# Expert stage: four token blocks by fetched rows and six dense, the low parts of u and v made on VectorE

## The chip, the cores and the metric

One of the eight cores of a Trainium2 chip runs the whole program, in fp32. Its engines are TensorE (PE; its weight loads are PEld), VectorE (DVE), ScalarE (ACT), GpSimd (POOL) and the queue of SyncE (SP) that issues transfers. The metric is the device time of one execution in microseconds (us), lower is better; the time before is the median of three runs.

## What is computed

An encoder block on 1280 tokens (256 of one request, 1024 of another) with 1024 features: norm, one projection, a two-way state-space branch, differential attention, a mix, and then PEER experts. The change is in the last part, whose reference is

```python
q = (xb @ w_q).reshape(tb, PEER_HEADS, 2, PEER_D_KEY // 2)          # 8 heads, 2 halves
s = jnp.einsum("thmd,mkd->thmk", q, sub_keys).astype(jnp.float32)   # 2 x 128 keys
s_top, i_top = lax.top_k(s, K)                                      # K = 16
...
best, pos = lax.top_k(cand, K)          # 16 of the 256 sums of a head
expert = jnp.take_along_axis(cand_idx, pos, axis=-1)                # one of 16384
gate = jax.nn.softmax(best, axis=-1)
ue = u[expert]
h = jax.nn.gelu(jnp.einsum("thkd,td->thk", ue, xb), approximate=False)
w = (gate * h).astype(xb.dtype)
return jnp.einsum("thk,thkd->td", w, v[expert])
```

Each token thus uses 8 x 16 = 128 of the 16384 experts; an expert is a row of u and a row of v, 1024 numbers each.

## The kernel before

The stages run one after another: `project`, `ssd`, `attention`, `mix`, `route` (finds each token's experts and gates), `spread_gates` and `experts`. The tokens are ten blocks of 128. In `experts` they are served in two ways side by side.

**Fetched rows.** The first `GB` = 3 blocks: for each of a token's 128 slots GpSimd issues an indirect DMA (`fetch`, L2363) that brings each of 128 tokens its own row, 128 x 1024 floats (512 KB), into one of `RB` = 6 buffers `row`. In the first half of the stage the rows are of u and VectorE makes a dot product of each with the token (`dot`, L2499); in the second half they are of v and VectorE adds each, weighted, to the token's result in `tok` (`blend`, L2510). 384 fetches for u and 384 for v.

**Dense.** The other `DB` = 7 blocks, `TD` = 896 tokens, go through all 16384 experts, 128 (one key k) at a time, two keys to a *period*, so 64 periods. TensorE multiplies u by x into `ph` (L2396), ScalarE takes the gelu (L2311), VectorE multiplies by the gates (`weights`, L2475), and TensorE multiplies that by v (`second_product`, L2418), into one of four banks `po`, 128 tokens x 512 features at a time (a *tile*, 14 to a period); VectorE adds the bank to `acc` (`add_output`, L2493). Two tiles of one block (`HELD`) stay in their own bank `held` over all periods. A period has four *quarters*: two keys by two spans of the tokens, of 512 and 384.

**Three products for one.** Each fp32 operand is split into a high part, which ScalarE rounds off by a copy (`split_u` L2294, `split_v` L2298, L2318 for w), and a low part, the rest, by a subtraction. Hence a first product of 8 x 3 matmuls a quarter and a tile of 2 x 3. The low parts of u and v are made by GpSimd (`rest_u` L2349, `rest_v` L2354: 128x1024 each, two of each per period), those of w by VectorE (`rest`, L2482). Each of u and v has one raw buffer (`u_raw`, `v_raw`): SP issues the next load (L2231, L2234) only when the low part is made. u has two split buffers, v four.

**What sets the order.** Every engine has its instructions written out by hand, period by period. TensorE's `period` puts the tiles between the matmuls of a quarter by numbers; VectorE's `period` puts rows (`row_work`), adds, `weights` and `rest` one behind another; GpSimd's loop puts `rest_u` and `rest_v` between fetches. Waits are on semaphores: `o_added` before a bank is written again, `w_lo`, `v_lo` and `u_lo` (low part there), `w_hi`, `u_hi` and `v_hi` (high part there), `row_used` before a row buffer is fetched into. ScalarE's quarter is: gelu, then (in quarters 1 and 3) `split_u` of the next key, then the high part of w. At the middle (`TURN` = period 32) the slots' gelu is taken, `tok` is loaded anew and blending begins.

**Before it**, `spread_gates` makes for the dense tokens the table of gates over all 16384 experts, for each block in 8 steps (56 in all, L2120), and stores 8192 KB for each block. `route` keeps the experts and gates of the first `GB` blocks in SBUF as well.

Of the kernel before, what the change touches and what calls it, by code (L numbers as in the profile page):

```python
# [6 lines left out]
F32 = mybir.dt.float32  # L21
U32 = mybir.dt.uint32
ALU = mybir.AluOpType
# [21 lines left out]
GB = 3  # L45
GT = GB * P
TD = T - GT
# [1957 lines left out]
def spread_gates(nc, c, routed, gates):  # L2005
# [10 lines left out]
    with ExitStack() as ctx:  # L2016
# [21 lines left out]
        with nc.Block() as block:  # L2038
# [85 lines left out]
            def _(act):  # L2124
# [35 lines left out]
                assert ROUNDS % STAGES == 0 and DB % 2  # L2160
# [4 lines left out]
                with act.Fori(1, DB // 2) as i:  # L2165
                    for b in range(2):
                        block_of(2 * i + b, b, i)
                block_of(DB - 1, 0, DB // 2, last=True)


def experts(nc, c, xn2_feat, h_tok, hn_tok, gates, gain2_row, expert_tok, gate_tok, u_exp, v_exp, u_rows, y):
# [3 lines left out]
    SPAN = ((0, 512), (512, TD - 512))  # L2175
# [3 lines left out]
    HELD = 5  # L2179
    ORING = 4  # L2180
    OT, RT = 2 * DB, 2 * (DB - 1)
    NEAR = 8
    RB = 6
# [4 lines left out]
    assert RT % ORING == 0 and RB % GB == 0  # L2188
    with ExitStack() as ctx:
# [18 lines left out]
        landing = [t[:, 0:TD] for t in (g[0], g[1], *row[1:RB], act_h)]  # L2208
# [17 lines left out]
        with nc.Block() as block:  # L2226
# [118 lines left out]
            def _(pool):  # L2345
# [5 lines left out]
                def rest_v(k):  # L2351
                    hi, lo = v[k % 4]
                    pool.wait_ge(v_hi, k + 1)
                    nc.gpsimd.tensor_tensor(lo[:], v_raw[:], hi[:].bitcast(F32), ALU.subtract).then_inc(v_lo, 1)  # L2354

                def fetch(r):

                    if r >= 2 * TOK_ROWS:
                        return
# [8 lines left out]
                rest_v(0)  # L2368
                pool.wait_ge(tok_scaled, GB)
                for r in range(RB):  # L2370
                    fetch(r)
                for p in range(PAIRS):
                    r0 = (2 * p + 1) * RB
                    if p:
                        rest_u(2 * p + 1)
                        rest_v(2 * p)
                    for r in range(0, 3):
                        fetch(r0 + r)
                    rest_v(2 * p + 1)
                    for r in range(3, 10):  # L2380
                        fetch(r0 + r)
                    if p + 1 < PAIRS:
                        rest_u(2 * p + 2)
                    for r in range(10, 12):
                        fetch(r0 + r)

            @block.tensor
            def _(pe):
# [12 lines left out]
                def second_product(p, t, odd, first, last):  # L2401
# [9 lines left out]
                    else:  # L2411
                        out = po[ring(t) % ORING][:]
# [30 lines left out]
                def period(p, odd, first=False, last=False):  # L2443
                    quarter(p, 0, odd, ((1, 7), (1, 8), (1, 9)), (4, 14, 6), first, last)
                    quarter(p, 1, odd, ((1, 10), (1, 11), (1, 12)), (8, 8, 8), first, last)
                    quarter(p, 2, odd, ((1, 13), (0, 0), (0, 1), (0, 2)), (4, 16, 2, 2), first, last)
# [259 lines left out]
```

## Time and profile before

| | |
|---|---|
| median of three runs (lowest to highest) | 5527.01 us (5522.74 to 5529.78) |
| span of the profiled execution | 5520.1 us |
| TensorE matmul busy | 4860.9 us, 88% of the span |
| VectorE busy | 3732.9 us, 68% |
| GpSimd busy | 2631.3 us, 48% |
| ScalarE busy | 1582.4 us, 29% |
| traffic | 861.24 MB, mean 156 GB/s |
| `experts` | from 3009.75 us on, 2510.3 us |
| `spread_gates`, its matmuls | 2714.0 to 2977.5 us |

The span is the time from the first to the last instruction of one execution; it stands 6.96 us under the median. "Busy" is the time in which an engine has an instruction in hand, and a matmul's end is modelled. A wait inside an instruction, such as for a port of the memory, counts as busy.

### The profile page before, as it was taken

Reading aid. Unit: us, or ns where it says so; the run is one execution under the profiler, and the core shown is the slowest. Engines: PE = TensorE matmul, PEld = TensorE weight load, DVE = VectorE, ACT = ScalarE, POOL = GpSimd, SP = SyncE. Lnnn points to the kernel's source line nnn. Section 1 sums busy time; section 2 is a strip of 40 time slices with the busy share of each in tenths; the row PEclk is TensorE's granted clock in tenths of the full one; section 3 lists DMA queues with packets and bytes.
Section 4 is the critical chain, followed back from the end, with each engine's and each line's share of the span. In section 5 each row is a group of like instructions: output and inputs, shape, how many; then the busy total and the mean of one; then the engine's idle time right before and its main releaser. Section 6 shows DMA issues by size and latency. Waiting matters only on the chain. (4 is left out here: it accounts for less than half of the span.)

```text
span 5520.1 us, 71031 instructions
## 1 busy us (share of the span) xinstructions
PE 4860.9 (88%) x24196; PEld 3924.5 (71%) x24196; DVE 3732.9 (68%) x7021; ACT 1582.4 (29%) x2809; POOL 2631.3 (48%) x1877
## 2 busy tenths in 40 slices
PE   7999995554999799765396999999999999999999
PEld 6888884443444486554285788888888888888888
DVE  2000003786578422889896888888888888888887
ACT  3111101554667421111396222222222221222221
POOL 4122210553345110344574666666666666666664
PEclk9999997777899899887698999999999999999999
DMA  3222211001311342000187777677777767677676
GB/s 128 85 85 85 83 50 61 28 25 50 132 50 57 119 145 87 30 33 20 38 230 242 282 241 247 233 247 239 244 243 244 252 235 245 239 244 244 234 249 214
DMA packets 356695, 861.24 MB, mean 156 GB/s; under 512 B 27032, under 2 KB 169144, under 8 KB 356280
## 3 DMA queue, kind: packets, MB, share of 16 engines
q1 hardware_dynamic: 235872, 414.54, 23.4%
q0 software_dynamic: 119552, 440.88, 22.3%
q10 hardware_dynamic: 1152, 4.46, 0.2%
q8 instruction: 47, 0.77, 0.1%
q14 instruction: 72, 0.59, 0.0%
HBM read 733.33 MB, written 125.14 MB: 156 GB/s over the span
## 5 line engine op out<-in xcount | busy, mean ns | idle before, releaser
L2396 PE MATMUL e_ph<-e_x,e_u 128*128 128x512 f32 (+1 forms) x6144 | 1381.7, 363 | 50.9 <-DVE e_x L2461 50.9
L2396 PEld LDWEIGHTS e_ph<-e_x,e_u 128*128 128x128 f32 x6144 | 1128.7, 188 | 219.5 <-issue 42.0
L2418 PE MATMUL e_po<-e_v,e_w 128*128 128x512 f32 x4608 | 1185.6, 393 | 10.5 <-POOL e_v L2354 10.5
L2418 PEld LDWEIGHTS e_po<-e_v,e_w 128*128 128x128 f32 x4608 | 859.9, 188 | 161.1 <-POOL e_v L2354 10.8
L338 PE MATMUL proj_acc<-xn,w_tile 128*128 128x512 f32 (+1 forms) x3456 | 677.7, 358 | 4.5 <-POOL w_tile L368 4.5
L2311 ACT ACTIVATE e_act<-e_ph 128x512 f32<-128x512 f32 (+1 forms) x256 | 139.6, 545 | 1820.7 <-PE e_ph L2396 1820.7
L338 PEld LDWEIGHTS proj_acc<-xn,w_tile 128*128 128x128 f32 x3456 | 575.0, 188 | 107.0 <-POOL w_tile L368 4.7
L2493 DVE TENSOR_TENSOR e_acc<-e_acc,e_po 128x512 f32<-128x512 f32 x768 | 516.9, 680 | 172.5 <-PE e_po L2418 172.5
L2510 DVE SCALAR_TENSOR_TENSOR e_tok<-e_row,e_slot,e_tok 128x1024 f32<-128x1024 f32 x384 | 586.4, 1540 | 1.9 <-DMA e_tok<-h_tok_dram 1.9
L2349 POOL TENSOR_TENSOR e_u<-e_u_raw,e_u 128x1024 fp32r<-128x1024 f32 x128 | 380.1, 2969 | 424.7 <-ACT e_u L2294 424.7
L2499 DVE SCALAR_TENSOR_TENSOR e_row<-e_row,e_tok 128x1024 f32<-128x1024 f32 x384 | 572.8, 1498 | 4.4 <-DMA e_row<-in_u_rows,expert_tok 4.4
L2363 POOL DMA_INDIRECT e_row<-in_v_exp,expert_tok x384 | 444.5, 1158 | 218.7 <-DVE e_tok L2510 137.9
L2363 POOL DMA_INDIRECT e_row<-in_u_rows,expert_tok x384 | 447.7, 1166 | 210.6 <-DVE e_row L2499 131.2
L298 DVE COPY proj_out<-proj_acc 128x1280 f32<-128x1280 f32 x25 | 37.3, 1492 | 659.1 <-PE proj_acc L338 646.3
L2482 DVE TENSOR_TENSOR e_w<-e_act,e_w 128x512 fp32r<-128x512 f32 (+1 forms) x256 | 430.4, 1681 | 4.8 <-ACT e_w L2318 4.8
L368 POOL TENSOR_TENSOR w_tile<-w_raw,w_tile 128x1024 fp32r<-128x1024 f32 x50 | 119.7, 2394 | 510.2 <-ACT w_tile L193 510.2
L2354 POOL TENSOR_TENSOR e_v<-e_v_raw,e_v 128x1024 fp32r<-128x1024 f32 x128 | 327.1, 2555 | 59.5 <-ACT e_v L2298 59.5
L1100 POOL TENSOR_SCALAR ex<-ex,sm 128x640 f32<-128x640 f32 (+1 forms) x80 | 192.4, 2405 | 196.1 <-DVE sm L1383 196.1
L2120 PE MATMUL g_acc<-g_second,g_first 128*128 128x128 f32 x1792 | 253.6, 289 | 26.7 <-DVE g_second L2106 25.7
L2120 PEld LDWEIGHTS g_acc<-g_second,g_first 128*128 128x128 f32 x1792 | 218.9, 193 | 61.6 <-DVE g_second L2106 45.4
L1694 POOL TENSOR_TENSOR r_hit<-r_hit,r_topf 128x2048 f32<-128x2048 f32 x20 | 90.2, 4510 | 351.8 <-DVE r_hit L1982 351.8
L1553 PE MATMUL mx_acc<-mx_src,mx_w 128*128 128x512 f32 (+1 forms) x1152 | 229.6, 360 | 27.7 <-DVE mx_src L1573 23.7
(312 smaller groups left out, 6880.1 us busy)
## 6 DMA issues: line engine op xcount, KB each, us to landing
e_u_raw<-in_u_exp SPq DMA_DIRECT2D x128, 512.0 KB, 4.0
e_v_raw<-in_v_exp SPq DMA_DIRECT2D x128, 512.0 KB, 3.5
gates_dram<-g_out SPq DMA_DIRECT2D x7, 8192.0 KB, 30.3
e_g<-gates_dram SPq DMA_DIRECT2D x128, 448.0 KB, 3.3
feat_dram<-proj_out POOLq DMA_DIRECT2D x50, 640.0 KB, 5.8
w_raw<-in_w_feat SPq DMA_DIRECT2D x50, 512.0 KB, 4.9
raw<-feat_dram SPq DMA_DIRECT2D x22, 640.0 KB, 6.0
mx_gate<-feat_dram SPq DMA_DIRECT2D x16, 640.0 KB, 4.0
```

The source lines that it names most:

```text
L338: last = nc.tensor.matmul(acc[b][:, s, 0:tn], w[b][p][:, k, :], xn[q][:, k, t0:t0 + tn], start=(k == 0 and i == 0), stop=(k == DC - 1 and ...
L1553: last = nc.tensor.matmul(acc[b][:, s, 0:tn], w[b][p][:, k, :], src[q][:, k, t0:t0 + tn], start=(k == 0 and i == 0), stop=(k == DC - 1 and ...
L2120: last = nc.tensor.matmul(acc[p][:, j, :], first[p][:, j, :], second[p][:, j, :], start=True, stop=True)
L2349: nc.gpsimd.tensor_tensor(whole(u[b][1]), u_raw[:], whole(u[b][0]).bitcast(F32), ALU.subtract).then_inc(u_lo, 1)
L2354: nc.gpsimd.tensor_tensor(lo[:], v_raw[:], hi[:].bitcast(F32), ALU.subtract).then_inc(v_lo, 1)
L2363: pool.indirect_dma_start(out=row[r % RB][:], out_offset=None, in_=u_rows if r < TOK_ROWS else v_rows, in_offset=bass.IndirectOffsetOnAxis ...
L2396: ins = nc.tensor.matmul(ph[q % 2][:, 0:tn], u[b][j][:, kk, :], xs[m][:, kk, t0:t0 + tn], start=(i == 0), stop=(i == 3 * DC - 1))
L2418: ins = nc.tensor.matmul(out, w[b][j][:, blk * P:(blk + 1) * P], v[2 * odd + b][m][:, half * HALF:(half + 1) * HALF], start=(n == 0 and (f ...
L2482: nc.vector.tensor_tensor(w[b][1][:, t0:t0 + tn], act_h[:, t0:t0 + tn], w[b][0][:, t0:t0 + tn].bitcast(F32), ALU.subtract).then_inc(w_lo, 1)
L2493: nc.vector.tensor_tensor(a, a, po[ring(t) % ORING][:], ALU.add).then_inc(o_added, 1)
L2499: nc.vector.scalar_tensor_tensor(out=row[m][:], in0=row[m][:], scalar=1.0, in1=tok[:, m % GB, :], op0=ALU.mult, op1=ALU.mult, accum_out=do ...
L2510: nc.vector.scalar_tensor_tensor(out=tok[:, m % GB, :], in0=row[m][:], scalar=slot[:, bass.ds(2 * RB * (p - TURN) + r, 1)], in1=tok[:, m % ...
```

## The change

`GB` becomes 4: 512 tokens by fetched rows, 512 fetches for u and 512 for v, and 16 rows instead of 12 to a period; `RB` becomes 8. `DB` becomes 6 (`TD` = 768): the spans are 384 and 384, a period has 12 tiles, of which 2 are held (`HELD` = 4), and `spread_gates` has 48 steps. GpSimd's loop is now fetches alone; `rest_u` and `rest_v` stand on VectorE, at places of their own in its period. A period's ten tiles that aren't held no longer fill the four banks a whole number of times, so the bank depends on the period's parity (`bank`), and VectorE's loops take two periods a round. On TensorE the tiles are put between the matmuls by new numbers. ScalarE and SP are as before.

```diff
-GB = 3
+GB = 4
@@ experts
-    SPAN = ((0, 512), (512, TD - 512))
+    SPAN = ((0, TD // 2), (TD // 2, TD // 2))
-    HELD = 5
+    HELD = 4
-    NEAR = 8
-    RB = 6
+    NEAR = DB
+    RB = 2 * GB
+    bank = lambda t, odd: (RT * odd + ring(t)) % ORING
@@ gpsimd
-                def rest_v(k):
-                    hi, lo = v[k % 4]
-                    pool.wait_ge(v_hi, k + 1)
-                    nc.gpsimd.tensor_tensor(lo[:], v_raw[:], hi[:].bitcast(F32), ALU.subtract).then_inc(v_lo, 1)
...
                 pool.wait_ge(tok_scaled, GB)
-                for r in range(RB):
+                for r in range(2 * TOK_ROWS):
                     fetch(r)
-                for p in range(PAIRS):
-                    r0 = (2 * p + 1) * RB
-                    if p:
-                        rest_u(2 * p + 1)
-                        rest_v(2 * p)
-                    for r in range(0, 3):
-                        fetch(r0 + r)
-                    rest_v(2 * p + 1)
-                    for r in range(3, 10):
-                        fetch(r0 + r)
-                    if p + 1 < PAIRS:
-                        rest_u(2 * p + 2)
-                    for r in range(10, 12):
-                        fetch(r0 + r)
@@ tensor
-                    quarter(p, 0, odd, ((1, 7), (1, 8), (1, 9)), (4, 14, 6), first, last)
+                    quarter(p, 0, odd, ((1, 4), (1, 5), (1, 6)), (4, 10, 10), first, last)
...
@@ vector
+                def rest_u(k, b):
+
+                    dve.wait_ge(u_hi, k + 1)
+                    nc.vector.tensor_tensor(whole(u[b][1]), u_raw[:], whole(u[b][0]).bitcast(F32), ALU.subtract).then_inc(u_lo, 1)
+
+                def rest_v(p, odd, b):
+
+                    hi, lo = v[2 * odd + b]
+                    dve.wait_ge(v_hi, 2 * p + b + 1)
+                    nc.vector.tensor_tensor(lo[:], v_raw[:], hi[:].bitcast(F32), ALU.subtract).then_inc(v_lo, 1)
+
...
-                    outputs(1, 6)
+                    outputs(1, 3)
+                    if not first and not last:
+                        rest_u(2 * p + 1, 1)
                     row_work(1)
-                    outputs(1, 7)
+                    outputs(1, 4)
+                    if not first and not last:
+                        rest_v(p, odd, 0)
                     row_work(2)
...
+                    row_work(5)
+                    if not last:
+                        rest_v(p, odd, 1)
...
+                    outputs(0, 0)
+                    if not last and more:
+                        rest_u(2 * p + 2, 0)
+                    row_work(14)
```

**VectorE at the border of two periods** (here of the first and the second, with the buffers' numbers). Before, from the last row of a period (`e_row5` into `e_dots1`) on:

```order
L2499 SCALAR_TENSOR_TENSOR e_row5,e_dots1<-e_row5,e_tok 128x1024
L2503 COPY e_slot<-e_dots1 128x6
L2493 TENSOR_TENSOR e_acc<-e_acc,e_po0 128x512
L2493 TENSOR_TENSOR e_acc<-e_acc,e_po1 128x512
L2475 TENSOR_TENSOR e_act<-e_act,e_g1 128x384
L2499 SCALAR_TENSOR_TENSOR e_row0,e_dots0<-e_row0,e_tok 128x1024
L2482 TENSOR_TENSOR e_w11<-e_act,e_w10 128x384
L2493 TENSOR_TENSOR e_acc<-e_acc,e_po2 128x512
L2499 SCALAR_TENSOR_TENSOR e_row1,e_dots0<-e_row1,e_tok 128x1024
```

Now, from the low part of the first u (`e_u01`) on:

```order
L2456 TENSOR_TENSOR e_u01<-e_u_raw,e_u00 128x1024
L2478 SCALAR_TENSOR_TENSOR e_row6,e_dots1<-e_row6,e_tok 128x1024
L2472 TENSOR_TENSOR e_acc<-e_acc,e_po1 128x512
L2478 SCALAR_TENSOR_TENSOR e_row7,e_dots1<-e_row7,e_tok 128x1024
L2482 COPY e_slot<-e_dots1 128x8
L2472 TENSOR_TENSOR e_acc<-e_acc,e_po2 128x512
L2443 TENSOR_TENSOR e_act<-e_act,e_g1 128x384
L2478 SCALAR_TENSOR_TENSOR e_row0,e_dots0<-e_row0,e_tok 128x1024
L2450 TENSOR_TENSOR e_w11<-e_act,e_w10 128x384
L2472 TENSOR_TENSOR e_acc<-e_acc,e_po3 128x512
L2456 TENSOR_TENSOR e_u11<-e_u_raw,e_u10 128x1024
```

Between the low parts of the two keys' u (`e_u01`, `e_u11`) stand three rows, three adds, one product with the gates and the low part of w; the copy of the dots comes every eight rows.

**GpSimd in a period** (here the last but one). Before:

```order
L2349 TENSOR_TENSOR e_u11<-e_u_raw,e_u10 128x1024
L2354 TENSOR_TENSOR e_v21<-e_v_raw,e_v20 128x1024
L2363 DMA e_row0<-in_v_exp,expert_tok 128x1024
L2363 DMA e_row1<-in_v_exp,expert_tok 128x1024
L2363 DMA e_row2<-in_v_exp,expert_tok 128x1024
L2354 TENSOR_TENSOR e_v31<-e_v_raw,e_v30 128x1024
L2363 DMA e_row3<-in_v_exp,expert_tok 128x1024
```

Now, the last eight of the program, as all of it:

```order
L2344 DMA e_row0<-in_v_exp,expert_tok 128x1024
L2344 DMA e_row1<-in_v_exp,expert_tok 128x1024
L2344 DMA e_row2<-in_v_exp,expert_tok 128x1024
L2344 DMA e_row3<-in_v_exp,expert_tok 128x1024
L2344 DMA e_row4<-in_v_exp,expert_tok 128x1024
L2344 DMA e_row5<-in_v_exp,expert_tok 128x1024
L2344 DMA e_row6<-in_v_exp,expert_tok 128x1024
L2344 DMA e_row7<-in_v_exp,expert_tok 128x1024
```

The subtractions are gone from GpSimd's queue, and a fetch there waits for `row_used` alone.

## Rows read from the trace of the kernel before

**Rows 1.** Stretch: us; busy PE, PEld, DVE, ACT, POOL; clock; DMA share; GB/s.

```profile
3118.00:4272.00 1154.00, 1154.00 (x5394) 992.45 (x5393) 1014.63 (x1379) 241.38 (x361) 746.65 (x481) 1.00 0.71 242
```

**Rows 2.** Chain that ended last, two pieces, a period apart (start us, us, what).

```profile
4080.79 3.17 PE e_ph L2396 x14
4119.31 3.17 PE e_ph L2396 x14
```

**Rows 3.** Timeline of TensorE: start us, us, line, operation, tiles, count.

```profile
3637.18 2.94 PE L2396 MATMUL e_ph<-e_x,e_u 128*128 128x384 f32 x16
3639.95 1.55 PE L2418 MATMUL e_po<-e_v,e_w 128*128 128x512 f32 x6
...
3645.86 1.55 PE L2418 MATMUL e_po<-e_v,e_w 128*128 128x512 f32 x6
3647.25 1.21 PE L2396 MATMUL e_ph<-e_x,e_u 128*128 128x384 f32 x6
```

**Rows 4.** Timeline of VectorE in the same period.

```profile
3623.59 1.21 DVE L2499 SCALAR_TENSOR_TENSOR e_row<-e_row,e_tok 128x1024 f32<-128x1024 f32 x1
...
3624.73 0.68 DVE L2493 TENSOR_TENSOR e_acc<-e_acc,e_po 128x512 f32<-128x512 f32 x1
3625.33 0.68 DVE L2475 TENSOR_TENSOR e_act<-e_act,e_g 128x512 f32<-128x512 f32 x1
...
3632.34 0.08 DVE L2499 DVE_READ_ACCUMULATOR e_row<-e_row,e_tok 128x1 f32 x1
...
3632.67 1.23 DVE L2499 SCALAR_TENSOR_TENSOR e_row<-e_row,e_tok 128x1024 f32<-128x1024 f32 x1
...
3645.77 2.75 DVE L2482 TENSOR_TENSOR e_w<-e_act,e_w 128x384 fp32r<-128x384 f32 x1
```

**Rows 5.** Timeline of GpSimd in that period.

```profile
3625.91 0.94 POOL L2363 DMA_INDIRECT e_row<-in_u_rows,expert_tok  x1 [0.30 <-issue]
...
3645.15 2.96 POOL L2349 TENSOR_TENSOR e_u<-e_u_raw,e_u 128x1024 fp32r<-128x1024 f32 x1 [3.47 <-ACT e_u L2294]
```

**Rows 6.** Timeline of VectorE: beside no GpSimd work; at the stage's start, three in 3.48 us.

```profile
5495.36 0.55 DVE L2482 TENSOR_TENSOR e_w<-e_act,e_w 128x384 fp32r<-128x384 f32 x1
...
3036.38 3.48 DVE L2465 TENSOR_TENSOR e_tok<-e_tok,e_row 128x1024 f32<-128x1024 f32 x3
```

**Rows 7.** Timeline of VectorE: a blend and what follows it.

```profile
4587.07 1.27 DVE L2510 SCALAR_TENSOR_TENSOR e_tok<-e_row,e_slot,e_tok 128x1024 f32<-128x1024 f32 x1
4588.26 0.68 DVE L2493 TENSOR_TENSOR e_acc<-e_acc,e_po 128x512 f32<-128x512 f32 x1
```

**Rows 8.** Timeline of ScalarE in the period of rows 4.

```profile
3644.02 1.05 ACT L2294 ACTIVATE e_u<-e_u_raw 128x1024 fp32r<-128x1024 f32 x1
3644.97 0.51 ACT L2318 ACTIVATE e_w<-e_act 128x384 fp32r<-128x384 f32 x1
```

**Rows 9.** Tile `e_u_raw`, 3100 to 5480 us: from issue to landing, 123 loads.

```profile
DMA to landing us min/median/max: 3.4/3.7/5.6
```

**Rows 10.** Transfers from 3060 to 3080 us: all, then an issue (KB, us to landing).

```profile
DMA packets 1840, 6.62 MB, mean 331 GB/s; under 512 B 205, under 2 KB 205, under 8 KB 1838
...
e_u_raw<-in_u_exp SPq DMA_DIRECT2D x1, 512.0 KB, 5.4
```

**Rows 11.** Transfers from 3618 to 4580 us: queues (packets, MB, share), then an issue.

```profile
q0 software_dynamic: 43199, 157.31, 46.4%
q1 hardware_dynamic: 21950, 76.77, 24.8%
...
e_tok<-h_tok_dram SPq DMA_DIRECT2D x1, 1536.0 KB, 7.2
```

**Rows 12.** Timeline of VectorE at the turn from dots to blends.

```profile
4278.79 1.28 DVE L2510 SCALAR_TENSOR_TENSOR e_tok<-e_row,e_slot,e_tok 128x1024 f32<-128x1024 f32 x1 [1.88 <-DMA e_tok<-h_tok_dram]
```

**Rows 13.** Tile `e_row`, 3100 to 5480 us: fetches of u rows, ns min/median/max.

```profile
L2363 POOL DMA_INDIRECT e_row<-in_u_rows,expert_tok x358: 932/1056/1769, 3100.3 to 4250.1; - x179
```

**Rows 14.** Timeline of TensorE in `spread_gates`: one of its 56 steps.

```profile
2952.82 4.53 PE L2120 MATMUL g_acc<-g_second,g_first 128*128 128x128 f32 x32 [0.17 <-DVE g_second L2106]
```

More of the change, by code:

```diff
@@ L2207, in experts @@
         po = [ps(f"e_po{q}", [P, HALF]) for q in range(ORING)]
-        landing = [t[:, 0:TD] for t in (g[0], g[1], *row[1:RB], act_h)]
+        landing = [t[:, 0:TD] for t in (g[0], g[1], *row[1:6], act_h)]
         assert len(landing) == DC
@@ L2492, in add_output @@
                     dve.wait_ge(o_done, OT * p + t + 1)
-                    nc.vector.tensor_tensor(a, a, po[ring(t) % ORING][:], ALU.add).then_inc(o_added, 1)
+                    nc.vector.tensor_tensor(a, a, po[bank(t, odd)][:], ALU.add).then_inc(o_added, 1)
                 def dot(p, r):
@@ L2520, in weigh_slots, with period @@
                     dve.wait_ge(slot_weighted, 1)
-                def period(p, first=False, second=False, blending=False, turning=False, last=False):
+                def period(p, odd, first=False, second=False, blending=False, turning=False, more=True, last=False):
                     def row_work(*rows):
@@ L2535, in outputs @@
                             if back and not first:
-                                add_output(p - 1, t, second)
+                                add_output(p - 1, t, 1 - odd, second)
                             elif not back and not last:
-                                add_output(p, t, first)
+                                add_output(p, t, odd, first)
                     if not first:
@@ L2574, in period @@
+                    row_work(10, 11)
+                    outputs(1, 11)
+                    row_work(12)
                     if not last:
                         weights(p, 2)
-                    row_work(10)
+                    row_work(13)
                     if not last:
                         rest(p, 2)
-                    outputs(0, 2, 3)
-                    row_work(11)
-                    outputs(0, 4, 5)
-                period(0, first=True)
-                period(1, second=True)
@@ L2585, in _ @@
-                with dve.Fori(2, TURN) as p:
-                    period(p)
-                period(TURN, blending=True, turning=True)
-                with dve.Fori(TURN + 1, PAIRS) as p:
-                    period(p, blending=True)
-                period(PAIRS, last=True)
+                    outputs(0, 0)
+                    if not last and more:
+                        rest_u(2 * p + 2, 0)
+                    row_work(14)
+                    outputs(0, 1)
+                    row_work(15)
@@ new lines, in period @@
+                    outputs(0, 2)
+                assert OT == 12 and 2 * RB == 16
+                period(0, 0, first=True)
+                period(1, 1, second=True)
+                with dve.Fori(1, TURN // 2) as i:
+                    for odd in range(2):
+                        period(2 * i + odd, odd)
+                period(TURN, 0, blending=True, turning=True)
+                period(TURN + 1, 1, blending=True)
+                with dve.Fori(TURN // 2 + 1, PAIRS // 2 - 1) as i:
+                    for odd in range(2):
+                        period(2 * i + odd, odd, blending=True)
@@ L2591, in _ @@
+                period(PAIRS - 2, 0, blending=True)
+                period(PAIRS - 1, 1, blending=True, more=False)
+                period(PAIRS, 0, last=True)
                 for half in range(2):
```

42 lines of the change are left out of this document (21 added, 21 removed).

## The prediction, as it was made before the changed kernel ran

> **What bounds the kernel now.** I first read the busy time by stretches. In `experts` TensorE is busy all of the time, 1154 us of 1154, at a granted clock of 1.00 (its level of 2.4 GHz); VectorE is busy 1014.63 us, 88% [rows 1]. The chain of waits then shows the same piece of TensorE's work every 4119.31 - 4080.79 = 38.52 us [rows 2]: that is a period, TensorE sets it, and 64 of them are 2466 of the stage's 2510 us. So the question is what TensorE needs after the change, and whether another engine, whose load grows, needs more.
>
> The timeline of VectorE explains its 88%. The low part of w on 384 columns takes 2.75 us beside GpSimd's low part of u, which runs from 3645.15 for 2.96 us [rows 4, 5]; with no GpSimd work beside it the same form takes 0.55 us [rows 6]. So a subtraction on GpSimd holds up a VectorE instruction that reads two tensors from SBUF. The Trainium skill (SBUF — State Buffer, "SBUF: two separate sides") calls the shared ports an exclusive lock for the whole of an instruction; by that rule, which this row agrees with, the wait goes with GpSimd's subtraction and not with its length on VectorE.
>
> **TensorE after the change.** Sixteen matmuls of 384 columns take 3639.95 - 3637.18 = 2.77 us, 0.173 each; a tile of six among them takes 3647.25 - 3645.86 = 1.39 us [rows 3]. A period is now 4 quarters x 24 = 96 matmuls of 384 columns, 16.6 us, and 12 tiles, 16.7 us: 33.3 us. If TensorE still bounds, a period falls by 5.2 us.
>
> **VectorE after the change**, start to start. A dot 3624.73 - 3623.59 = 1.14 us; an add 0.60 [rows 4]; a blend 1.19 [rows 7]; the keeping of eight dots 3632.67 - 3632.34 = 0.33 [rows 4]; the product with the gates and the low part of w on 384 columns 0.55 less the overlap of 0.07 that the others show, 0.48 [rows 6]. The low parts of u and v are not in the trace on this engine; the nearest row is the scaling of `tok`, two SBUF tensors of 128x1024, three in 3.48 us, hence 1.14 us each start to start [rows 6]. I take that; the form doesn't go below it, and one blend's 1.19 is the upper end. A dense-and-dot period is 16 x 1.14 = 18.2, two keeps 0.7, ten adds 6.0, eight products and low parts of w 3.8, four low parts of u and v 4.6: 33.3 us. A blending one has 19.0 for rows and no keeps: 33.4 us. The same count of the kernel before gives 12 x 1.14 + 0.7 + 12 x 0.60 + 4 x 0.60 + 4 x 0.48 = 25.9 us against 38.52 x 0.88 = 33.9 that rows 1 show: 8.0 us of it is waiting behind GpSimd's four subtractions, which goes away. VectorE thus takes on four rows and four subtractions at no more than its old busy time, but the period shrinks onto it: both engines now need 33.3 to 33.4 us, with no slack.
>
> **What is late next: the load of u.** At the border of two periods VectorE makes the low part of u's first key, then three rows, two adds, a keep, one product with the gates, and then the low part of w, which waits for ScalarE's high part. That cover is 3 x 1.14 + 2 x 0.60 + 0.33 + 0.48 = 5.4 us. The freed `u_raw` is loaded again meanwhile, and on ScalarE the split of the new u stands ahead of the high part of w. The chain is the passing on between engines (two of the 0.17 that rows 14 show), the load L, the split 0.95 (start to start) and the high part 0.51 [rows 8], so L + 1.8, and VectorE stands L + 1.8 - 5.4 = L - 3.6 us a period. By the loads' median of 3.7 us that is 0.1, by the longest of 5.6 it is 2.0 [rows 9]. Before, GpSimd had the low part of u on a queue with room, and VectorE never stood for this. In blending the cover has no keep and longer rows, 0.2 us less.
>
> L will be above the old median, since the traffic thickens. A period now moves 16 rows of 524 KB = 8.39 MB, u and v 2.10 MB, gates 0.79 MB: 11.3 MB in 34.5 us, 327 GB/s, where it was 242 [rows 1]. The one stretch that ran at such a rate, 331 GB/s, had its u landing after 5.4 us [rows 10]; but there GpSimd was issuing fetches back to back, while now each waits for a row to be used. I take the middle of 3.7 and 5.4, L = 4.6, and so a wait of 1.0 us with dots and 1.2 with blends. Periods: 33.3 + 1.0 = 34.3 and 33.4 + 1.2 = 34.6, mean 34.5 us. Over 64 periods: 64 x (38.52 - 34.5) = 257 us saved. The fetches themselves are hidden: VectorE uses one row in some 2.1 us, so eight buffers give about 14 us for a fetch and its landing.
>
> **The rest.** `spread_gates` runs a step in 4.53 + 0.17 = 4.70 us [rows 14]; 8 steps go, 38 us saved, on the path, since nothing of `experts` begins before its end. The turn costs more: VectorE stood 1.88 us for `tok` [rows 12], whose 1536 KB landed after 7.2 us [rows 11]; the 524 KB more need 1.6 us at the 331 GB/s of rows 10, the low part of w ahead of it is 2.3 us shorter, and this time nothing gives it back: 5 us. The last periods' leftover is eight tiles instead of seven, 1.4 us. One more scaling of `tok` and one more block of gates kept in `route`, 2.3 us together at 1.14 each. Together 9 us lost; below nothing I see none of these. The new banks, numbers between the tiles and TensorE's waits on `o_added` I cost at nothing, as TensorE has 1.2 us to spare in a period of 34.5.
>
> **Sum.** 5520.1 - 257 - 38 + 9 = 5234 us of span, and 7 to the median: **5241 us**. This case alone is 5205 to 5275 (periods of 34.0 to 35.0).
>
> **Rivals.** (a) *No wait for u.* L stays at its median of 3.7, and periods are 33.4 to 33.8: 64 x 4.9 = 314 saved, 5520 - 314 - 38 + 9 + 7 = 5184. For it: the fetches are evenly spread; against it: the rate of traffic, and that two engines at their limit with waits across seldom meet the larger of the two.
>
> (b) *The transfers bound.* Rows took 446 us of DMA time for 157.31 MB and the other loads 239 us for 76.77 MB (46.4% and 24.8% of 962 us) [rows 11]. By these 8.39 MB cost 23.8 and 2.88 MB 9.0 us: 32.8 us of a period, and at 331 GB/s [rows 10] the 11.3 MB need 34.1. So a period below 34 may be out of reach, and near that limit loads land late. With L = 5.6 the wait for u is 2.0 us, and the second v, loaded between two low parts of v with four rows, two adds and two short ones between (6.7 us, against L + 1.4), begins to cost 0.3: 35.7 to 36, 64 x 2.7 = 173 saved, 5325. The Trainium skill (HBM Reference, "Access") gives a core about 358 GB/s where both cores of a pair stream and about 425 where one does. By 358 a period would need 31.5 us and wouldn't be bound, and the 331 of rows 10 is below either figure.
>
> (c) *GpSimd's fetches bound.* The hold-up may work both ways: a fetch takes 932 ns at best and 1769 at most [rows 13], with 0.30 to the next [rows 5], and VectorE now reads two SBUF tensors most of the time. At the median of 1.06 a period's 16 take 22 us, at the longest 33 us, which is still within the period; where each first waits out a whole dot of 1.22 and then takes 0.93, it is 16 x 2.45 = 39.2 us, no gain. Halfway between the last two, 36.2 us, it saves 64 x 2.3 = 149: 5349. Against it: half of the fetches were at 1.06 or less though VectorE was busy 88% of that time as well.
>
> (d) *Slower than before.* The single `u_raw` and `v_raw` decide: with both waits a period loses L - 3.6 and L - 5.3 us, and it is longer than 38.52 + 0.6 (what the rest gives back, and the margin) once L passes 7.4 us, which no load of u reached in 123 [rows 9]. At L = 8, 40.4 us a period: 5520 + 120 - 38 + 9 + 7 = 5618.
>
> **Chances.** The forecast 0.48, (a) 0.20, (b) 0.22, (c) 0.07, (d) 0.03. The range that holds 8 in 10 takes in (a) and most of (b): 5178 to 5335. Faster by over 0.2% (about what a measurement tells from no change, 11 us) 0.96, within 0.01, slower 0.03.
>
> **What would show it.** TensorE's matmul pieces should be those of rows 3, but with gaps of about 1 us a period, before a tile that waits for VectorE; VectorE should be busy 96% or more of a stretch like that of rows 1, with its low part of w at 0.55 us and that of u at 1.2. Its one wait should be the low part of w of quarter 3, released by ScalarE, and ScalarE's `split_u` should have waited for the load. GpSimd should be below 75% busy. The prediction is wrong if low parts on VectorE take more than 1.3 us, if its instructions still show 2.7 us beside fetches, if TensorE shows gaps for banks, or if the period's length follows bytes and not VectorE's sum.

## The result

| | before | after |
|---|---|---|
| median of four runs | 5528.3 us | 5388.9 us (5382.4 to 5394.9) |
| ratio, 95% interval | 1 | 0.975 (0.974 to 0.976) |
| span of the profiled execution | 5520.1 us | 5382.7 us |

The kernel is faster by 139 us, where 286 were forecast. The time lies above the range's upper end of 5335: the sign was right, and the gain about half of the forecast.

### The profile page after: what moved, and what is told of

It reads as the page before. It is cut to its first block and busy times, and to the rows that moved or that the text cites. A ratio compares the mean times of both kernels' runs of the same rounds, so it can differ in the third digit from the quotient of the medians.

```text
span 5382.7 us, 69055 instructions
## 1 busy us (share of the span) xinstructions
PE 4569.1 (85%) x23172; PEld 3724.8 (69%) x23172; DVE 3662.7 (68%) x7429; ACT 1526.6 (28%) x2729; POOL 2223.2 (41%) x1840
## 5 line engine op out<-in xcount | busy, mean ns | idle before, releaser
L2364 PE MATMUL e_ph<-e_x,e_u 128*128 128x384 f32 x6144 | 1220.7, 340 | 61.9 <-DVE e_x L2429 52.5
L2386 PE MATMUL e_po<-e_v,e_w 128*128 128x512 f32 x3840 | 1019.0, 401 | 156.6 <-DVE e_w L2450 144.6
L2386 PEld LDWEIGHTS e_po<-e_v,e_w 128*128 128x128 f32 x3840 | 714.1, 190 | 305.6 <-issue 176.2
L2344 POOL DMA_INDIRECT e_row<-in_v_exp,expert_tok x512 | 607.0, 1185 | 581.6 <-DVE e_tok L2489 527.5
L2344 POOL DMA_INDIRECT e_row<-in_u_rows,expert_tok x512 | 595.5, 1163 | 569.8 <-DVE e_row L2478 522.9
L2306 ACT ACTIVATE e_w<-e_act 128x384 fp32r<-128x384 f32 x256 | 133.5, 521 | 1142.6 <-DVE e_act L2443 1142.6
L2472 DVE TENSOR_TENSOR e_acc<-e_acc,e_po 128x512 f32<-128x512 f32 x640 | 433.0, 677 | 4.7 <-PE e_po L2386 4.7
L2450 DVE TENSOR_TENSOR e_w<-e_act,e_w 128x384 fp32r<-128x384 f32 x256 | 140.8, 550 | 213.2 <-ACT e_w L2306 213.2
L2282 ACT ACTIVATE e_u<-e_u_raw 128x1024 fp32r<-128x1024 f32 x128 | 135.0, 1055 | 519.8 <-DMA e_u_raw<-in_u_exp 519.8
L1539 PEld LDWEIGHTS mx_acc<-mx_src,mx_w 128*128 128x128 f32 x1152 | 191.9, 189 | 65.4 <-issue 16.7
```

Of the source, the lines that this page charges most:

```text
L1539: last = nc.tensor.matmul(acc[b][:, s, 0:tn], w[b][p][:, k, :], src[q][:, k, t0:t0 + tn], start=(k == 0 and i == 0), stop=(k == DC - 1 and ...
L2306: nc.scalar.activation(w[b][0][:, t0:t0 + tn], act_h[:, t0:t0 + tn], ACT.Copy).then_inc(w_hi, 1)
L2344: pool.indirect_dma_start(out=row[r % RB][:], out_offset=None, in_=u_rows if r < TOK_ROWS else v_rows, in_offset=bass.IndirectOffsetOnAxis ...
L2364: ins = nc.tensor.matmul(ph[q % 2][:, 0:tn], u[b][j][:, kk, :], xs[m][:, kk, t0:t0 + tn], start=(i == 0), stop=(i == 3 * DC - 1))
L2386: ins = nc.tensor.matmul(out, w[b][j][:, blk * P:(blk + 1) * P], v[2 * odd + b][m][:, half * HALF:(half + 1) * HALF], start=(n == 0 and (f ...
L2450: nc.vector.tensor_tensor(w[b][1][:, t0:t0 + tn], act_h[:, t0:t0 + tn], w[b][0][:, t0:t0 + tn].bitcast(F32), ALU.subtract).then_inc(w_lo, 1)
```

## The profile after

The page of the changed kernel has these lines: busy time, the queues with bytes and share, the chain's share by engine, and the issues with KB and us to landing.

```profile
PE 4569.1 (85%) x23172; PEld 3724.8 (69%) x23172; DVE 3662.7 (68%) x7429; ACT 1526.6 (28%) x2729; POOL 2223.2 (41%) x1840
...
q0 software_dynamic: 156416, 575.12, 29.3%
q1 hardware_dynamic: 218688, 397.83, 22.2%
...
DVE 23%; DMA 9%; issue 6%; PE 4%; DVEq 1%; ACT 1%; POOL 0%; ACTq 0%; SPq 0%
...
e_u_raw<-in_u_exp SPq DMA_DIRECT2D x128, 512.0 KB, 6.6
e_v_raw<-in_v_exp SPq DMA_DIRECT2D x128, 512.0 KB, 5.0
```

TensorE hardly shows in the chain now; VectorE and DMA do. The loads of u land after 6.6 us, where 3.7 was the median [rows 9]. Both are medians over two loads a period; the second of them, on which the wait below hangs, is taken apart further on. By stretches (us; busy PE, PEld, DVE, ACT, POOL; clock; DMA share; GB/s), as in [rows 1]:

```profile
3500.00:4000.00 500.00, 469.96 (x2297) 414.83 (x2296) 451.64 (x765) 103.93 (x162) 256.35 (x221) 0.99 0.86 309
4500.00:5000.00 500.00, 468.00 (x2283) 411.45 (x2282) 455.69 (x518) 103.81 (x161) 258.30 (x219) 0.99 0.85 306
```

Nobody is busy all of the time any more: TensorE 94%, VectorE 90 to 91%, GpSimd 51%, the DMA engines 85 to 86%. When three engines all sit just below full, one should look for a wait that goes round between them. The chain names its link. In most periods it holds one piece of about 7 us of the same kind (start us, us, what). Here are two of them from the half with dots, 17 periods apart; 13 more stand between them, and in three periods the chain takes another way:

```profile
3258.32 7.17 DMA e_u_raw<-in_u_exp
...
3882.88 7.08 DMA e_u_raw<-in_u_exp
```

(3882.88 - 3258.32) / 17 = 36.7 us a period; in the blending half the same pieces come every 36.9 us. The waits from 3200 to 4100 us (who waited, for what, us in total, times, longest) and the timelines of one border between two periods give the rest.

```profile
ACT e_u L2282 <- DMA e_u_raw<-in_u_exp: 176.8, 24, 7.8
DVE e_w L2450 <- ACT e_w L2306: 77.3, 24, 3.9
PE e_po L2386 <- DVE e_w L2450: 54.1, 43, 2.2
```

VectorE:

```profile
4028.00 1.21 DVE L2456 TENSOR_TENSOR e_u<-e_u_raw,e_u 128x1024 fp32r<-128x1024 f32 x1
...
4033.41 1.22 DVE L2478 SCALAR_TENSOR_TENSOR e_row<-e_row,e_tok 128x1024 f32<-128x1024 f32 x1
4034.55 0.08 DVE L2478 DVE_READ_ACCUMULATOR e_row<-e_row,e_tok 128x1 f32 x1
4037.43 0.56 DVE L2450 TENSOR_TENSOR e_w<-e_act,e_w 128x384 fp32r<-128x384 f32 x1 [2.79 <-ACT e_w L2306]
```

SyncE's queue, then ScalarE, then TensorE:

```profile
4029.47 0.33 SPq L2219 DMA_DIRECT2D e_u_raw<-in_u_exp  x1
```

```profile
4035.93 1.06 ACT L2282 ACTIVATE e_u<-e_u_raw 128x1024 fp32r<-128x1024 f32 x1 [7.04 <-DMA e_u_raw<-in_u_exp]
4036.89 0.50 ACT L2306 ACTIVATE e_w<-e_act 128x384 fp32r<-128x384 f32 x1
```

```profile
4038.12 1.65 PE L2386 MATMUL e_po<-e_v,e_w 128*128 128x512 f32 x6 [1.41 <-DVE e_w L2450]
```

Read across: VectorE has finished the low part of u at 4029.14 (the next instruction starts there), SyncE issues the next load at 4029.47, it lands 6.4 us later, ScalarE splits it at 4035.93 and only then makes the high part of w, and VectorE, ready since 4034.63, goes on at 4037.43. That is the wait which the prediction named, where it named it, with its law: 6.4 - 3.6 = 2.8 us. Its length is not: 77.3 / 24 = 3.2 us a period with dots and 85.1 / 25 = 3.4 with blends, not 1.0 and 1.2.

## Experiments: what the wait is worth, and where it can be hidden

The theory after the result: the period is 33.3 us plus the wait for u, and everything hangs on L, the time from issue to landing. The rival: at these bytes the transfers are the bound, and taking the wait away would only turn it into another one.

**e1_u_early.** VectorE makes the low part of the first u after row 11, three rows sooner, so that `u_raw` comes free sooner.

```diff
                     row_work(10, 11)
+                    if not last and more:
+                        rest_u(2 * p + 2, 0)
                     outputs(1, 11)
...
                     outputs(0, 0)
-                    if not last and more:
-                        rest_u(2 * p + 2, 0)
```

> The changed kernel, with one line of VectorE's period moved: the low part of the next period's first u (which frees u_raw for the load of the second) stands behind row 11 instead of behind the first tile's add after row 13, some 4.4 us earlier. Theory (wait for the load of u): in the changed kernel VectorE stands 3.2 us a period for ScalarE's high part of w, which stands behind a split that waits for a load of u that takes 6.6 us. With 4.4 us more cover the wait goes: periods of 33.4 to 34.2 instead of 36.9 us, and 5389 - 64 x 3.0 = about 5195 us (5175 to 5220). Rival (bytes): the 11.3 MB of a period can't pass faster than the 305 GB/s of now, so the wait comes back at the rows: within 15 us of 5389. Rival in between (the load lengthens as the period shrinks): 5230 to 5320.

Measured: 5312.6 us, 0.961 (0.960 to 0.963). That is in the range of the third expectation, but its reason is the smaller part: the load that matters takes 0.4 us longer than in the changed kernel, and above all it starts late. VectorE freed `u_raw` sooner but the load didn't go. VectorE, then SyncE's queue:

```profile
4829.47 1.21 DVE L2456 TENSOR_TENSOR e_u<-e_u_raw,e_u 128x1024 fp32r<-128x1024 f32 x1
...
4832.39 0.54 DVE L2443 TENSOR_TENSOR e_act<-e_act,e_g 128x384 f32<-128x384 f32 x1
```

```profile
4833.10 0.33 SPq L2225 DMA_DIRECT2D e_g<-gates_dram  x1
4833.69 0.33 SPq L2219 DMA_DIRECT2D e_u_raw<-in_u_exp  x1
```

u is free at 4830.6 and its load is issued 3.1 us later, because SyncE first waits for the product with the gates (L2443) to reload `g`. Here an instruction that waits in SyncE's queue holds up by 3.1 us one behind it that is ready.

**e2_g_behind.** SyncE alone: the second load of u stands ahead of that of the gates.

```diff
-                    sp.wait_ge(wt_done, NQ * p + 3)
-                    load_g(2 * p + 2, 0)
                     sp.wait_ge(u_lo, 2 * p + 3)
                     load_u(2 * p + 3)
+                    sp.wait_ge(wt_done, NQ * p + 3)
+                    load_g(2 * p + 2, 0)
```

> The changed kernel with two loads of SP exchanged: the second u of the next period is issued before the gates of its first key, which in the changed kernel stand ahead of it by 3.4 us in the same queue and are still under way (6.7 us to landing). If the queue ahead makes the load of u long: it lands after some 5.0 instead of 6.4 us and the wait of 3.2 us falls to about 1.8: 5389 - 64 x 1.4 = about 5300 us. If the fetched rows make it long, by sharing the DMA engines: it lands after 6 us or more and the time is within 30 us of 5389.

Measured: 5379.8 us, 0.973 (0.972 to 0.975), no more than 9 us from the changed kernel, with intervals that overlap. u still landed after 6.3 us and VectorE stood as before (`e_w` released by ScalarE, 77.0 us in 24 times). So it is not the gates' place in front of u that makes it late. The run does not acquit their 393 KB altogether: they are now issued 0.7 us behind u, where they were 3.4 us ahead of it.

**e7_early_all.** Both edits together.

> Both edits of the first two runs together: the low part of the next first u behind row 11, and SP's load of the second u ahead of the load of gates. In the run with the first edit alone u_raw was free at 4830.7 us, but SP issued the load at 4833.7, since it stood in order behind a load of gates that waits for VectorE's product after row 12; so only 1.4 of the 4.4 us of cover arrived (76 us gained). Theory (wait for the load of u): now the cover grows by the other 3.0 us, the wait of some 2 us a period goes, periods are 33.4 to 34.0 us, and the time is 5312 - 64 x 2 = about 5185 us (5170 to 5225). Rival (traffic: 11.3 MB a period at no more than 320 GB/s, 35.2 us): it stays within 15 us of 5312.

Measured: 5194.7 us (5193.0 to 5196.4), 0.940 (0.939 to 0.942). Stretches as above:

```profile
3250.00:4000.00 750.00, 750.00 (x3778) 679.06 (x3777) 743.53 (x1261) 180.24 (x270) 391.08 (x361) 1.00 0.93 338
4400.00:5100.00 700.00, 688.96 (x3442) 618.07 (x3441) 685.82 (x779) 162.82 (x246) 446.61 (x328) 1.00 0.91 330
```

With dots TensorE is busy 750 of 750 us again, VectorE 99%: the period of 33.3 us that the prediction counted is real, and the DMA engines carry it at 338 GB/s. The rival falls. Its lower limit of 34.1 us a period came from 331 GB/s, which was what was asked for in [rows 10], not what could be had. The Trainium skill (HBM Reference, "Specifications (TRN2)", where the figures of the prediction stand too) puts one streaming core at about 425 GB/s and at about 358 where both of a pair stream; 338 is below either, so this run doesn't tell the two apart. In the blending half 1.6% is missing: VectorE waits there for the split of the second v, 14.2 us in 21 times.

**e9_v_later.** To e7 is added that the low part of the second v stands one row and one add further back, to give its load more cover.

```diff
-                    row_work(5)
+                    row_work(5, 6)
+                    outputs(1, 7)
                     if not last:
                         rest_v(p, odd, 1)
-                    row_work(6)
-                    outputs(1, 7)
```

> The two moves of the seventh run (u's low part behind row 11, its load ahead of the gates), and the second low part of v one row and one add later, behind tile 7's. Theory: in the blending half of that run VectorE still stood 0.6 us a period for a load of v of 6.5 us, which has a cover of 6.7 less some 1.4; with 1.8 us more cover this goes, and the dot half, which TensorE bounds at 33.3, stays: 5195 - 32 x 0.6 = about 5176 us (5168 to 5188). Rival (TensorE and VectorE are so even that any wait gone is made good by another): within 5 us of 5195.

Measured: 5185.5 us (5185.2 to 5189.4), 0.939 (0.937 to 0.941): the lowest median here, 203 us below the changed kernel, though its interval overlaps that of e7. The wait for v is gone from the blending half; in its place VectorE now and then waits for a row itself:

```profile
DVE e_tok L2489 <- DMA e_row<-in_v_exp,expert_tok: 11.2, 8, 2.6
```

u lands after 6.8 us in this kernel, no sooner than in the changed one, and it costs nothing: what counts is the cover, not the landing. What is near its limit in the blending half is now GpSimd. From 4400 to 5100 us its 330 fetches take 535 us, 1.62 us each, and 225 of them follow the one before without waiting for a row to be used; its fetches are 23% of the chain there.

**e8_early_w_first.** All three edits together, e7's two and that of e4 below, gave no time: with them the waits of VectorE, ScalarE and TensorE close a circle and the program does not end. Which wait closes it was not traced.

**e4_w_first.** The other way round: ScalarE makes the high part of w ahead of the split of u in quarters 1 and 3, so that a late u no longer holds w.

```diff
-                        if s == 1 and more:
-                            split_u(2 * p + 2 + b, b)
                         act.wait_ge(wt_done, NQ * p + q + 1)
...
                         nc.scalar.activation(w[b][0][:, t0:t0 + tn], act_h[:, t0:t0 + tn], ACT.Copy).then_inc(w_hi, 1)
+                        if s == 1 and more:
+                            split_u(2 * p + 2 + b, b)
```

> The changed kernel with two instructions of ScalarE exchanged: the high part of w of quarters 1 and 3 stands ahead of the split of u instead of behind it. Theory: the low part of w no longer waits for a load; the next in VectorE's order that does is the low part of the second u itself, 1.1 us later in its period and without the 0.5 us of the high part of w and 0.5 of the split's lead: the wait falls from 3.2 to about 1.2 us a period, 5389 - 64 x 2.0 = about 5260 us (5240 to 5290). Rival (the load lands later still, or the rows' traffic bounds): within 30 us of 5389.

Measured: 5296.3 us, 0.958 (0.957 to 0.960), just above the expected 5240 to 5290. VectorE's wait has moved one step on, to its own low part of u, and is 46.3 / 25 = 1.9 us a period instead of 3.2:

```profile
DVE e_u L2456 <- ACT e_u L2282: 46.3, 25, 2.6
```

That wait has a low part of w and an add more to cover it, 1.1 us, and no high part of w in its chain, 0.5: 1.6 us less by that, 1.3 measured. So the order on ScalarE was less than half of the wait, and the rest is L as before (6.7 us).

## Experiments: why u lands late

**Two loads a period.** The wait hangs on one of a period's two loads of u, the second, which is issued alone at the border; the first is issued 0.6 us behind a load of v. [rows 9] and the medians so far mix them. For the second alone (medians over 22 to 27 loads, from 3200 to 4100 us with dots and from 4400 to 5300 with blends), with the mean number of fetched rows that were issued over 0.1 us before it and had not landed:

| kernel | rows on the way, dots / blends | second u lands after, us |
|---|---|---|
| before | 0 / 0 | 3.5 / 3.5 |
| e6 | 1.0 / 1.0 | 4.6 / 4.6 |
| e5 | 2.0 / 2.0 | 4.9 / 4.4 |
| changed | 3.0 / 3.0 | 6.9 / 7.0 |
| e10 | 3.0 / 3.0 | 6.9 / 6.9 |
| e12 | 0.8 / 0.9 | 3.5 / 3.5 |
| e1 | 3.0 / 2.0 | 7.3 / 7.3 |
| e7 | 3.3 / 2.5 | 6.0 / 3.6 |
| e9 | 4.0 / 3.5 | 7.3 / 6.5 |

e1, e7 and e9 are described above, the others follow.

**e6_three_blocks.** Three fetched blocks and seven dense ones as before the change, with the low parts of u and v on VectorE: that half of the change alone, with the order between the tiles as before.

```diff
-GB = 4
+GB = 3
...
-    SPAN = ((0, TD // 2), (TD // 2, TD // 2))
+    SPAN = ((0, 512), (512, TD - 512))
```

> The other part alone: the sizes of before (three blocks by rows, seven dense), with the low parts of u and v on VectorE, the second low part of v behind row 4, that of the next first u behind the add of tile 2. Theory: TensorE bounds at 38.5 us a period either way, VectorE falls from 88% to 30.5 of 38.5 us, 79%: the time is that of before, within 15 us of 5528. Rival (the single raw buffer costs a wait even here): a load of 3.7 to 5.4 us with a cover of 0.6 + 3 x 1.14 + 0.33 + 0.6 + 0.48 = about 5 us plus what VectorE waits for TensorE anyway: up to 1 us a period, 5590 us.

Measured: 5527.7 us, 1.0004 (0.9994 to 1.0014). Its stretch, and the landing of `e_u_raw` (both loads) from 3100 to 5480 us:

```profile
3250.00:4000.00 750.00, 750.00 (x3510) 645.46 (x3510) 599.63 (x975) 157.96 (x233) 244.65 (x234) 1.00 0.75 242
```

```profile
DMA to landing us min/median/max: 4.2/4.9/7.8
```

TensorE bounds, as in [rows 1], and VectorE has fallen from 88% to 80% although it does four more operations a period: the 8 us of lock wait are gone. And at the same 242 GB/s as before, u lands after 4.9 us instead of the 3.7 of [rows 9], the second u after 4.6 instead of 3.5. Nothing was added to the traffic; what was taken away is GpSimd's subtraction, and with it the fetches moved: one is now on the way, issued 2.1 us ahead of the load.

**e5_pool_parts.** The other half alone: four fetched blocks, the subtractions left on GpSimd.

```diff
+                for p in range(PAIRS):
+                    r0 = (2 * p + 1) * RB
+                    if p:
+                        rest_u(2 * p + 1)
+                        rest_v(2 * p)
+                    for r in range(0, 4):
+                        fetch(r0 + r)
+                    rest_v(2 * p + 1)
...
+                    if p + 1 < PAIRS:
+                        rest_u(2 * p + 2)
```

> One part of the change alone: four blocks by rows and six dense, but the low parts of u and v stay on GpSimd (two subtractions, four fetches, one subtraction, nine fetches, one subtraction, three fetches a period). Theory: VectorE's own work is 33.3 - 4.6 = 28.7 us, and four subtractions of GpSimd hold it up for 8 us: 36.7 us at least, and GpSimd needs 4 x 2.7 + 16 x 1.4 = 33 us and more with its own waits: periods of 37 to 39 us, 5390 to 5520 us. Rival (the hold-up is small or hidden in VectorE's slack): periods near TensorE's 33.3 to 34.5, about 5240 us.

Measured: 5477.7 us, 0.991 (0.989 to 0.993). Its stretch, and the landing of `e_u_raw` in the same 3100 to 5480 us:

```profile
3250.00:4000.00 750.00, 685.35 (x3342) 604.00 (x3341) 720.36 (x1037) 153.14 (x236) 637.03 (x398) 0.99 0.85 298
```

```profile
DMA to landing us min/median/max: 3.8/4.5/7.7
```

The time is as expected, but with dots it is not VectorE that bounds. It is busy 96% of the time with less work than in the changed kernel, and holds its dots for 1.58 us on average instead of 1.21, so the lock keeps its price. GpSimd, though, has no slack. These are its waits in the same stretch, and the shares of the chain there:

```profile
POOL e_row L2351 <- issue: 86.2, 306, 0.3
POOL e_u L2337 <- ACT e_u L2282: 22.6, 19, 1.8
```

```profile
by line: POOL e_row L2351 45.7%; DMA e_u_raw<-in_u_exp 12.8%; POOL e_v L2342 12.5%; POOL e_u L2337 12.1%; issue 10.7%; DVE e_row L2499 2.7%; ACT e_u L2282 2.6%; DVE e_acc L2493 0.7%; SPq L2219 0.2%; DVE e_act L2464 0.1%; DVE e_w L2471 0.1%;
```

Its 637 us of work, the 0.30 us between two fetches and the wait for a split of u fill 746 of 750 us: a period of 37.8 us is GpSimd's 16 fetches and four subtractions, and a load of u. Moving the subtractions thus gave time on two engines at once.

And the second u lands after 4.9 and 4.4 us at 298 and 293 GB/s, where the changed kernel has 6.9 and 7.0 at 307 and 305, while e6 and the kernel before differ at the same 242. So the mean rate alone does not tell the landing: the pauses of GpSimd count as well, and so do the added rows. One look back into the trace before shows what a pause did there (GpSimd, then SyncE; the subtraction is the one a period ahead of that in [rows 5]):

```profile
3602.22 0.94 POOL L2363 DMA_INDIRECT e_row<-in_u_rows,expert_tok  x1 [0.81 <-DVE e_row L2499]
3606.70 2.95 POOL L2349 TENSOR_TENSOR e_u<-e_u_raw,e_u 128x1024 fp32r<-128x1024 f32 x1 [3.55 <-ACT e_u L2294]
3609.81 1.09 POOL L2363 DMA_INDIRECT e_row<-in_u_rows,expert_tok  x1 [0.16 <-issue]
```

```profile
3609.82 0.33 SPq L2231 DMA_DIRECT2D e_u_raw<-in_u_exp  x1
```

GpSimd waits for the split and then subtracts, 7.6 us without a fetch, and the subtraction itself is what sets the load of the second u free. The row fetched at 3602.22 landed after 5.3 us, 2.3 us before that load was issued, so it found no row left. (At the period's other pair of loads, v at 3622.15 and the first u at 3622.73, it is plainer still: two subtractions stand back to back and the DMA engines move 0 GB/s from 3619.47 to 3622.47.) In the changed kernel the DMA share is 0.91 in the microsecond ahead of the load at 4029.47, with five fetches issued in the 8.5 us before it. The last three of them did not wait for a row to be used, but followed one another:

```profile
4024.76 1.44 POOL L2344 DMA_INDIRECT e_row<-in_u_rows,expert_tok  x1 [0.30 <-issue]
4026.50 1.31 POOL L2344 DMA_INDIRECT e_row<-in_u_rows,expert_tok  x1 [0.30 <-issue]
4028.12 1.91 POOL L2344 DMA_INDIRECT e_row<-in_u_rows,expert_tok  x1 [0.30 <-issue]
```

**e3_half_rows** (a single run). The blends fetch half a row each.

> The changed kernel, but in the second half of the stage each fetch brings 512 instead of 1024 floats a token, and each blend adds this half row twice (left out: the other half of v's rows; the work of VectorE is the same in count and length). Bytes of a blending period fall from 11.3 to 7.1 MB. Theory (the rows' traffic on the shared DMA engines makes the load of u take 6.6 us): in the second half u lands after about 4 us, the wait of 3.2 us falls below 1, periods from 37 to 34.2, and 32 x 2.8 = 90 us go: about 5300. The first half stays at 36.8 a period. Rival (the load is long for another reason, such as its place in SP's queue): both halves alike, within 20 us of 5389.

Measured: 5323.6 us. In the blending half, 4400 to 5100 us, with whole rows in the changed kernel and then with half rows:

```profile
DMA to landing us min/median/max: 4.9/6.6/7.7
```

```profile
DMA to landing us min/median/max: 3.7/5.2/5.8
```

Fewer bytes of rows bring u sooner by 1.4 us, the second u alone from 7.0 to 5.0, and VectorE's wait falls by the same 2.0 us, from 3.4 to 28.5 / 20 = 1.4. The direction is that of the theory; I had expected L nearer to 4.

**e10_hold_rows.** Is it the rows issued beside the load or those ahead of it? From the 15th row of a period's 16 on, GpSimd waits until u has landed.

```diff
+                    p, at = divmod(r - RB, 2 * RB)
+                    if r >= RB and at == 14 and p < PAIRS - 1:
+                        pool.wait_ge(u_in, 16 * (2 * p + 4))
```

> The changed kernel with one wait more on GpSimd: once a period, when VectorE has used the last row but one before it comes to the border, GpSimd holds the next fetch until the load of the second u has landed. Nothing is moved on VectorE, SP or ScalarE, and a row held back is used only some 13 us later. Theory (the load of u takes 6.4 us only because fetches are issued beside it; before, GpSimd's own subtraction kept them back just then): u lands after 3.5 to 4.5 us, VectorE's wait falls from 3.3 to about 1 us a period, and 5389 - 64 x 2.3 = about 5240 us (5200 to 5280). Rival (the load is long by the mean rate of traffic, 308 GB/s, or by the gates ahead of it): it stays above 6 us and the time within 20 us of 5389, or above.

Measured: 5414.1 us, 0.980 (0.979 to 0.982), slower than the changed kernel. GpSimd, then SyncE:

```profile
4004.71 1.90 POOL L2347 DMA_INDIRECT e_row<-in_u_rows,expert_tok  x1 [0.31 <-issue]
4013.45 0.94 POOL L2347 DMA_INDIRECT e_row<-in_u_rows,expert_tok  x1 [6.84 <-DMA e_u_raw<-in_u_exp]
```

```profile
4006.06 0.33 SPq L2219 DMA_DIRECT2D e_u_raw<-in_u_exp  x1
```

No fetch starts beside the load (the last one is in hand until 4006.61), and it still lands after 6.6 us. The theory that it is late only because of the fetches issued beside it falls. Six fetches had gone out in the 9.2 us ahead of it.

**e12_hold_sooner.** The same wait three rows sooner (`at == 11`), so that what was issued has drained when the load goes.

> As the run that held a fetch until the second u had landed (5414 us; there u still took 6.6 us though no fetch was issued beside it), but the hold begins three rows sooner, some 5 us ahead of the load. Theory (a load waits for what was issued before it: at its issue some four rows of 524 KB and the gates stood in the queues, 2.5 MB, 6 us at 400 GB/s; before the change GpSimd's subtraction had left the queues empty then): u now lands after 3.5 to 4.5 us, and VectorE's wait for the high part of w falls from 3.3 to about 1 us a period; the rows held back may cost some of it again: 5230 to 5330 us. Rival (the load is long by its place in SP's queue or the address it reads): u stays above 6 us, and the time at 5414 or above.

Measured: 5283.2 us, 0.956 (0.955 to 0.958). GpSimd, SyncE and ScalarE:

```profile
4016.02 0.94 POOL L2347 DMA_INDIRECT e_row<-in_u_rows,expert_tok  x1 [0.30 <-issue]
4026.03 1.83 POOL L2347 DMA_INDIRECT e_row<-in_u_rows,expert_tok  x1 [9.06 <-DMA e_u_raw<-in_u_exp]
```

```profile
4018.47 0.33 SPq L2225 DMA_DIRECT2D e_g<-gates_dram  x1
4021.88 0.33 SPq L2219 DMA_DIRECT2D e_u_raw<-in_u_exp  x1
```

```profile
4025.29 1.06 ACT L2282 ACTIVATE e_u<-e_u_raw 128x1024 fp32r<-128x1024 f32 x1 [3.99 <-DMA e_u_raw<-in_u_exp]
```

With the last fetch 5.9 us ahead of the load, u lands in 3.4 us, as early as before the change, at 320 GB/s on average. The gates stand 3.4 us ahead of it as in the changed kernel, so they alone do not make it late either. It is with rows already on the way that it comes late. How many is not the whole of it: in e7's blending half 2.5 are on the way and the second u lands after 3.6 us, in e1's there are 2.0 and it lands after 7.3. The hold costs something too: the fetches are made up for in a burst, the period's other load of u then takes 9.1 us and v 7.0, and VectorE waits for v instead:

```profile
DVE e_v L2465 <- ACT e_v L2286: 39.0, 25, 2.3
```

That is 1.6 us a period, so emptying the queue is the worse cure here; e7 and e9 leave the backlog and issue the load sooner.

## Why the prediction was off, step by step

- **What bounds, and what TensorE needs: right.** e7 shows the 33.3 us with TensorE at 750 of 750.
- **The lock wait and VectorE's sum: right.** A low part of u measured 1.14 us start to start, that of w lasts 0.55 us, and the 99% of e7 at the 33.3 us period is VectorE's 33.3. The Trainium skill's rule (SBUF — State Buffer, "SBUF: two separate sides") that the shared ports are locked for a whole instruction agrees with both halves of the change: e6 gives the 8 us back at the old load, and e5 keeps them at the new one (a dot of 1.58 us and a low part of w of 1.00 on average, for 1.22 and 0.55 in e6).
- **The wait for u, its place and its law L - 3.6: right.** 6.4 - 3.6 = 2.8, and 2.79 measured.
- **L itself: wrong, and this is the miss.** I took the middle of 3.7 and 5.4, L = 4.6; the second u took 6.9 us with dots and 7.0 with blends. The law then gives waits of 3.3 and 3.6 us, measured 3.2 and 3.4. Periods are 36.8 us and not 34.5: 64 x 2.3 = 147 us of a miss of 5382.7 - 5234 = 149, and the 2.3 us are those of L. VectorE's share, 96% or more in the forecast, fell to 90% with them. The number failed in its premises. The 3.7 of [rows 9] is a median over two loads of different kind (3.5 for the second, 4.3 for the first), and neither is a landing at 242 GB/s as such: the second u found no row on the way, because GpSimd's subtraction had held the fetches back, and the change removes the subtraction. And my argument against the 5.4 of [rows 10], that a fetch now waits for a row to be used, does not hold where it matters: the last three fetches ahead of the load go out one behind another. I read medians and the queue's mean share and not the moment of issue.
- **`spread_gates`: right.** Its matmuls' first and last start:

```profile
L2106 PE MATMUL g_acc<-g_second,g_first x1536: 275/275/550, 2714.8 to 2940.4; 128*128 128x128 f32 x192
```

  225.6 us, where 2714.0 to 2977.5 was 263.5: 38 less, as forecast.
- **The turn: nearly right.** VectorE stands 6.06 us for `tok`; the forecast counted 1.88 + 1.6 + 2.3 = 5.8 and put it at 5.
- **The sum, remade:** 5520.1 - 64 x (38.52 - 36.8) - 38 + 9 = 5381, measured 5382.7.
- **The rivals.** (a), no wait for u, is what e7 and e9 made of the kernel: 5195 and 5186, for 5184, though by more cover and not by its L of 3.7. (b), 5325, had the better L of 5.6, but its reason fell, since bytes did not bound up to 338 GB/s. (c) gave 5349, the nearest time, by luck: in the changed kernel GpSimd is busy 51% and mostly waits for rows to be used. It is no empty rival, though: fetches are much of what bounds e5, and they are on the chain of e9's blending half. (d) did not come; the wait for the second v, which was part of both (b) and (d), shows in e7 and e12. It is open why the longest loads take 8 us and more, and how much of a load's time each row ahead of it costs; no run here had a different number of rows on the way and nothing else different.
- **The range.** It took L from 3.7, the old median, to 5.6, the longest of the old trace. Where the surroundings of a load change, its old times are no bounds; with 6.9 and 7.0, the formula as written gives periods of 36.6 and 37.0 us, and so 5388.

## What to carry to other kernels

A landing time belongs to one load and to the moment of its issue: before using a median, take the load apart that the wait hangs on, look at what was on its way when it was issued, and ask whether the change keeps that. Work taken off an engine that also issues transfers removes pauses in its stream, and here a load that shares the DMA engines paid for it (3.5 to 4.6 us by that alone). With a single landing buffer on the critical round, free it sooner and put its load first in its queue, both together: apart they gave 76 and 9 us (the 9 within the intervals), together 194.

## What was unexpected of the hardware

- The same 512 KB load took 3.4 us with the last fetch 5.9 us back (e12) and 6.6 us with six in the 9.2 us before and none started beside it (e10). In one kernel, e7, it took 6.0 us with 3.3 rows on the way and 3.6 with 2.5.
- One core sustained 338 GB/s over 750 us, mixed of fetched rows and plain loads, at a DMA share of 0.93, with TensorE busy all of the time at a granted clock of 1.00, its level of 2.4 GHz (e7, e9); windows of 1 us in e12 reach 421 GB/s.
- GpSimd's fetches take 0.94 us or, like those shown of e10 and e12, up to 1.9, and 1.62 on average in e9's blending half, where they reach the chain. Whether VectorE's instructions hold them up was not tried apart.
